# Two attention mixers woven into one list of steps: differential heads in pairs, a pair's neighbourhood tile between them, and other engine orders around it

## The reference

```python
zl = yl @ w_in; zc = yc @ w_in              # 9 groups of 256 columns
# pool: windowed mean, product with pool_w;  conv: gate, 31 taps, layernorm, silu, product with pw
# "diff": 4 heads, each two softmaxes of width 32
q, k = axial_rope(q) * scale, axial_rope(k)  # latent tokens alone
p = softmax(q @ [kl, kc].T)                  # 768 keys; 256 for context queries
o = (p[2h] - lam * p[2h+1]) @ v[h]           # v of width 64; then an rmsnorm per head
# "na": 4 heads of width 64, neighbourhood attention on the 8 x 64 grid
s = [q @ kl.T + bias (banded, -1e30 outside), q @ kc.T]
o = softmax(s) @ [vl, vc]
out = concat(pool, conv, diff, na) @ w_out
```

## Time and profile before

| | |
|---|---|
| median of 3 runs | 3031.3 us (3029.96 to 3033.0) |
| the profiled execution | 3028.46 us, of which the span 3026.8 us |
| granted PE clock over the span | 0.962 of 2.4 GHz |
| PE busy, DVE busy, ACT busy, POOL busy | 94%, 57%, 28%, 10% |
| layer 0: attention from its second step to mix_out | 835 to 1046 us |
| layer 1: the same | 2438 to 2591 us |

### The profile page before, as it was taken

The page is one execution under the profiler, slowest core; times in us unless marked ns, Lnnn a source line. Parts: engine busy times, 40 slices in busy tenths (PEclk is TensorE's granted clock), DMA queues, the critical chain, the costliest instruction groups (busy, mean ns, idle before and its releaser), DMA issues.

```text
span 3026.8 us, 39917 instructions
## 1 busy us (share of the span) xinstructions
PE 2851.0 (94%) x14770; PEld 2547.3 (84%) x14770; DVE 1723.1 (57%) x2888; ACT 856.7 (28%) x1147; POOL 291.6 (10%) x279
## 2 busy tenths in 40 slices
PE   6999999999779999999999899999998879999998
PEld 6999999979643489999999799999987844678887
DVE  7676677669663457666676772222247664533334
ACT  3221122241363332211221422112232264432222
POOL 0000000014322100000000100000004332000000
PEclk8999999999877999999999999999998979999999
DMA  5333333321220012332333232111212220123232
GB/s 202 118 118 123 114 118 132 108 75 55 62 61 7 18 52 98 131 130 93 132 123 120 76 112 74 59 63 62 72 47 91 67 66 7 56 83 105 89 98 83
DMA packets 63375, 264.95 MB, mean 88 GB/s; under 512 B 8880, under 2 KB 11824, under 8 KB 53680
## 3 DMA queue, kind: packets, MB, share of 16 engines
q1 hardware_dynamic: 50608, 180.17, 18.2%
q0 software_dynamic: 11520, 75.11, 7.6%
q10 hardware_dynamic: 1152, 8.39, 0.7%
HBM read 252.89 MB, written 2.10 MB: 84 GB/s over the span
## 4 chain that ended last, share of the span: by engine, by line
PE 82%; DVE 11%; ACT 4%; issue 2%; DMA 1%; POOL 0%; ACTq 0%; SPq 0%; DVEq 0%
PE ps L1453 73%; PE ps L1692 2%; DVE conv_acc L1206 2%; PE ps L1619 2%; PE ps L1647 1%; PE ps L1627 1%; DVE w_lo L954 1%; DVE rstd L1007 1%; DVE nmax L1311 1%; ACT e_sb L866 1%; DVE y_hi L1043 1%; DMA x<-in_xT 1%; DVE y_lo L1045 1%; ACT probs_t L880 1%; DVE mod_start_acc L1388 1%
## 5 line engine op out<-in xcount | busy, mean ns | idle before, releaser
L1453 PE MATMUL ps<-y_hi,w_hi 128*128 128x384 f32 (+2 forms) x3184 | 905.2, 347 | 66.2 <-DVE y_lo L1035 32.5
L1453 PE MATMUL ps<-y_hi,w_lo 128*128 128x384 f32 (+2 forms) x3184 | 893.8, 344 | 0.0
L1453 PE MATMUL ps<-y_lo,w_hi 128*128 128x384 f32 (+2 forms) x3184 | 893.3, 344 | 0.0
L1453 PEld LDWEIGHTS ps<-y_hi,w_hi 128*128 128x128 f32 x3184 | 582.5, 190 | 108.6 <-DVE y_lo L1035 36.9
L645 ACT ACTIVATE w_hi<-w_raw 128x1024 fp32r<-128x1024 f32 (+1 forms) x290 | 326.7, 1128 | 1048.7 <-PE ps L1453 1048.7
L1453 PEld LDWEIGHTS ps<-y_lo,w_hi 128*128 128x128 f32 x3184 | 585.9, 189 | 22.5
L1453 PEld LDWEIGHTS ps<-y_hi,w_lo 128*128 128x128 f32 x3184 | 585.7, 190 | 20.9 <-issue 0.2
L954 DVE TENSOR_TENSOR w_lo<-w_raw,w_hi 128x1024 fp32r<-128x1024 f32 (+1 forms) x290 | 386.5, 1333 | 311.7 <-ACT w_hi L645 308.5
L969 DVE SCALAR_TENSOR_TENSOR mod_acc<-mod_raw,cact,mod_acc 128x256 f32<-128x256 f32 x896 | 360.0, 477 | 0.0
L1453 PE MATMUL ps<-h_hi,w_hi 128*128 128x384 f32 (+2 forms) x1254 | 354.1, 342 | 0.0
L1453 PE MATMUL ps<-h_lo,w_hi 128*128 128x384 f32 (+2 forms) x1254 | 351.4, 339 | 0.0
(11 more groups left out here) (162 smaller groups left out, 2032.0 us busy)
## 6 DMA issues: line engine op xcount, KB each, us to landing
w_raw<-in_w_up SPq DMA_DIRECT2D x176, 512.0 KB, 3.5
mod_raw<-in_w_mod POOLq DMA_DIRECT2D x64, 1024.0 KB, 5.1
w_raw<-in_w_down SPq DMA_DIRECT2D x64, 704.0 KB, 4.1
w_raw<-in_w_in SPq DMA_DIRECT2D x36, 512.0 KB, 3.5
mod_start<-in_w_mod ACTq DMA_DIRECT2D x8, 1024.0 KB, 22.0
w_raw<-in_w_out SPq DMA_DIRECT2D x16, 512.0 KB, 3.5
stack<-qk_hi SPq DMA_DIRECT2D x48, 96.0 KB, 2.1
band<-in_rpb POOLq DMA_DIRECT2D x16, 224.0 KB, 6.5
```

The source lines that it names most:

```text
L1453: mm = pe.matmul(slot[s][:, at:at + b - a], w[s][:, k, :], r[:, k, a:b], start=(k == 0 and n == 0), stop=(k == kc - 1 and n == 2))
```

## The change

It redraws the mixer in both layers:

- `attention_steps` weaves: for each pair of heads c, the rows of queries in turn; each row gives a step of diff head 2c, one of diff head 2c+1, and one of the na pair c. The last two na rows of a pair follow at its end. An na step is now two heads and one tile. The counts of steps (36 and 24) and of turned tiles (48 and 32) stay.
- na scores (`near_scores`) alternate the two heads, which lie on partitions 0 to 63 and 64 to 127, and come behind the step's turns and value products on PE. Diff scores stay ahead of them.
- Value products (`weigh_values`) are made per pair of heads and tile, three steps behind, 128 queries at a time; the two heads write PSUM partitions 0 to 63 and 64 to 127 in turn. The probabilities lie in a ring of four tiles. ACT copies each result out (`copy_out`, now 24 and 16 small copies in place of 4 and 4 large ones).
- DVE takes a step's first maximum ahead of the last step's reciprocals.
- `Z_ORDER` makes NA_V, NA_K, NA_Q the last units in that order. DVE's rotary steps move from units 15 and 16 to units 9 and 11, with fewer taps there (`TAPS`); the na scaling moves behind the value copies.
- The high parts of diff chunks 0 and 2 are made on ACT ahead of unit 14, `qk_lo` of them on POOL ahead of the bands' masks, and head 0's stacks can go out during mix_in. Head 1's wait for the turned values, head 2's and 3's for the last scores of heads 0 and 1.
- The convolution's root, reciprocal, norm, silu and pointwise product and the pool product move into the steps. So do the first four `y_hi`.

```diff
 def attention_steps(with_ctx):
-    for h in range(HEADS):
-        tiles = [(t, False) for t in range(LAT // P)] + [(t, True) for t in range(CTX // P)] * with_ctx
-        out += [("diff", h, (t,), c, n == len(tiles) - 1) for n, (t, c) in enumerate(tiles)]
-    for h in range(HEADS):
-        tiles = [((0, 1), False), ((2, 3), False)] + [((0, 1), True)] * with_ctx
-        out += [("na", h, t, c, n == len(tiles) - 1) for n, (t, c) in enumerate(tiles)]
+    rows = [(t, False) for t in range(LAT // P)] + [(t, True) for t in range(CTX // P)] * with_ctx
+    for c in range(WC):
+        near = [("na", c, t, ctx) for t, ctx in rows]
+        for n, (t, ctx) in enumerate(rows):
+            out += [("diff", 2 * c, t, ctx), ("diff", 2 * c + 1, t, ctx)]
+            if n < len(rows) - 2:
+                out.append(near[n])
+        out += near[len(rows) - 2:]
     return out
...
+Z_ORDER = [CONV_A // 2, CONV_G // 2, POOL_U // 2, DIFF_Q // 2, DIFF_K // 2, DIFF_V // 2, NA_V // 2, NA_K // 2, NA_Q // 2]
+QK_AT = 7
+TAPS = (5, 6, 6, 6, 6, 6, 1, 6, 1, 6, 6, 6, 1)
...
             def stack_heads(layer):
                     if h == 1:
-                        sp.wait_ge(sems["conv_pw"], WC * (layer + 1))
+                        sp.wait_ge(sems["v_turned"], (layer + 1) * (TOK // P))
                     if h >= 2:
-                        sp.wait_ge(sems["scores"], scored + (h - 1) * per_head)
+                        sp.wait_ge(sems["scores"], scored + 2 * last_step(layer, "diff", h - 2) + 2)
+                    if h == 3:
+                        sp.wait_ge(sems["conv_pw"], WC * (layer + 1))
...
             def mix_in(p):      # DVE
-                    if u >= 3:
-                        convolve(6)
-                    if u == 15:
+                    if u >= 3 and u - 3 < len(TAPS):
+                        convolve(TAPS[u - 3])
+                    if u == 9:
...
                 for k in range(len(steps) + 3):      # DVE
+                    if k < len(steps):
+                        maxima(k, 0)
                     if 1 <= k <= len(steps):
                         invert_sums(k - 1)
-                    if k < len(steps):
-                        maxima(k, 0)
                     if k < len(steps):
                         maxima(k, 1)
                     if 1 <= k <= len(steps):
                         scale_probs(k - 1)
+                    if 1 <= k <= parts:
+                        if k == 1:
+                            t.wait("conv_sqrt")
+                        part = slice(CTX * (k - 1), CTX * k)
+                        dve.reciprocal(rstd[:, part], rstd[:, part]).then_inc(sems["conv_rstd"], 1)
...
+                def near_scores(k):      # PE
+                    kind, c, tile, ctx = steps[k]
+                    for a, b in spans(TOK)[1 if ctx else 0:]:
+                        for s in range(2):
+                            if a == 0 or ctx:
+                                t.wait("exp")
+                            rows = slice(DH * s, DH * s + DH)
+                            mm = pe.matmul(slot[s][:, a:b], z[rows, NA_Q + c, at:at + P], z[rows, NA_K + c, a:b],
+                                           start=True, stop=ctx or a > 0)
...
+                        for s in range(2):
+                            mm = pe.matmul(slot[s][:, 0:LAT], backward[:, :], bands[2 * c + s][:, j:j + GRID_H, :], start=False, stop=True)
+                            mm.then_inc(sems["scores"], 1)
...
+                def weigh_values(k):
+                    pe.wait_ge(sems["probs_t"], 2 * n_pair + 2)
+                    at = 512 * (n_pair % 2)
+                    for n_key, key in enumerate(keys):
+                        for s in range(2):
+                            col = (0 if kind == "diff" else W) + DH * (2 * c + s)
+                            mm = pe.matmul(outs[DH * s:DH * s + DH, at:at + P], v_sb[:, key, col:col + DH],
+                                           ring[(2 * n_pair + s) % 4][:, n_key, :], start=(n_key == 0), stop=(key == TOK // P - 1))
+                    mm.then_inc(sems["pv"], 1)
...
                     for s in range(2):
-                        if k < len(steps):
-                            scores(k, s)
-                        if turned and s < len(turned[2]):
+                        if k < len(steps) and not near:
+                            diff_scores(k, s)
+                        if turned and s < tiles_of(turned):
                             transpose_probs(k - 2, s)
-                            tiles_turned += 1
-                    if k == 0:
-                        conv_pointwise()
+                    if closed and closes_pair(closed):
+                        weigh_values(k - 3)
+                    if near:
+                        near_scores(k)
+                    if k < WC:
+                        pool_product(k)
+                    if k - pointwise_at in range(WC):
+                        conv_pointwise(k - pointwise_at)
```

More of the change, by code:

```diff
@@ L568, in mixer @@
+                low_parts((0, 2))
                 t.wait("band_raw", 16 * 2 * (HEADS - 1))
-                for h in range(HEADS - 1):
+                for h in (0, 1, 3):
                     for row in range(2):
                         mask_band(h, row)
[L573 to L577, removed]
@@ new lines, in mixer @@
+                steps = attention_steps(layer < LAYERS - 1)
+                for k, (kind, h, tile, ctx) in enumerate(steps):
+                    if k == last_step(layer, "diff", 1):
+                        pool.wait_ge(sems["stacked1"], 16 * 12 * (2 * layer + 1))
+                        load_band(2)
+                    if k == last_step(layer, "diff", 1) + 3:
+                        t.wait("band_raw", 16 * 2)
+                        mask_band(2, 0)
+                    if k == last_step(layer, "diff", 1) + 4:
+                        mask_band(2, 1)
@@ L869, in copy_probs @@
[L869 to L881 removed]
+                qk_hi_part(layer, 1)
@@ L1331, in scale_probs @@
                 def scale_probs(k):
-                    kind, h, tiles, ctx, _ = steps[k]
+                    kind, h, tile, ctx = steps[k]
                     keys = slice(LAT, TOK) if ctx else slice(0, TOK)
@@ L1367, in mixer @@
+                for first, c in norm_from.items():
+                    for j in range(parts):
+                        if first + j >= len(steps) + 3:
+                            if j == 0:
+                                t.wait("head_sqrt")
+                            head_norm(c, slice(CTX * j, CTX * j + CTX))
+                dve.wait_ge(sems["turned"], turned_before(layer + 1))
                 for m in range(DC):
                     t.wait("y_hi")
+                    if m == DC // 2:
+                        dve.wait_ge(sems["pv"], turned_before(layer + 1) // 2)
@@ L1596, in scores, with conv_pointwise @@
-                def scores(k, s):
-                    kind, h, tiles, ctx, _ = steps[k]
+                def conv_pointwise(m):
+                    if m == 0:
+                        t.wait("conv_act", WC)
+                    pe.wait_ge(sems["probs_t"], made[0])
+                    for a, b in spans(n):
+                        for c in range(WC):
+                            mm = pe.matmul(turn[:, a:b], pw_sb[:, c, P * m:P * m + P], (act_buf, hid_buf)[c][:, a:b],
+                                           start=(c == 0), stop=(c == WC - 1))
+                    mm.then_inc(sems["conv_pw"], 1)
@@ L1621, in scores @@
-                    if band:
-                        if tile == 0:
-                            t.wait("band_ready")
-                        j = GRID_H - 2 - 2 * tile
-                        mm = pe.matmul(slot[s][:, 0:LAT], backward[:, :], bands[h][:, j:j + GRID_H, :], start=False, stop=True)
-                    mm.then_inc(sems["scores"], 1)
-                steps = attention_steps(with_ctx)
-                pe.wait_ge(sems["rope_done"], layer + 1)
-                heads, norm_at, sqrt_at, pv_from = 0, None, None, None
```

490 lines of the change are left out of this document (238 added, 252 removed).

## The result

The changed kernel took 3065.8 us (median of 4 runs, 3064.2 to 3069.3), the kernel before 3032.1 us beside it: a ratio of 1.0119, 95% interval 1.0104 to 1.0134. It is slower by 34 us where 66 us of gain were predicted. The profiled execution has a span of 3062.5 us against 3026.8: 35.7 us to find.

A forecast was written before the change was run, and what follows sets the result against it. Diff steps were taken as bound by a two-slot loop, na steps by nearly full PE. Gains of 42.1 us (layer 0) and 24.6 (layer 1), 66.7 together, took 3028.5 to 2961.8, 2965 us on the median's footing; range 2925 to 3022.

The forecast's parts named there:

- G: Time of one woven latent triple (diff, diff, na): 9.8 + 2P + S = 14.3 us, 15.8 with surcharge; break-even at 20.0.
- 0.5 us for that score: First part of the triple: second diff step's second score, two turns of 0.67 us and two sets of value products.
- S: Both heads' na scores in a triple: 1.7 us with overlap in PE's array, 2.98 one after another.
- 6.0 us of slot loop: Rest of the triple after the bands: scores, maxima, copies and exponentials of two diff steps passing through two PSUM slots.
- I cost it at nothing: DVE's maximum ahead of reciprocals: a late na score delays reciprocals wanted two steps later; nothing, or 0.4 us a triple uncovered.
- surcharge of 1.5 us on G: Share for queueing and slow clock, a tenth or more as in the old na steps, raising 14.3 to 15.8 us.
- 8 in each layer: Count of woven latent triples, entering both layers' sums as 8G = 126.4 us.
- start of attention: Earlier rotary steps, value turns and stacks bring step 1's scores forward: 18.7 us gained in layer 0, 12.7 in layer 1.
- P: A pair's value products, 24 passes of 128 columns: 1.4 us with overlap in PE's array, 2.7 one after another.
- rival without overlap: Opposite halves of PE's array run one after another: G 18.2 to 19.7 us, total 3003 to 3027 us; chance 0.22.
- stall at the change to heads 2 and 3: Scores wait for stack transfers on SP's queue in layer 0: 1 us for head 2 and 4 for head 3.
- slower rival: Short value products no longer lift PE's clock: G up to 23.6 us; about 3057 us at G = 21.7; chance 0.08.

The follow-up runs named there:

- sums first: The changed kernel with DVE's order alone put back, the last step's reciprocals ahead of the step's first maximum: 3052.0 us, ratio 1.0075.

## Why the prediction was wrong

**The step that failed** is the size of G, the woven triple, and in it first the line that begins "0.5 us for that score" and ends "The copies and scalings that these wait for fit between them". It counts from the second diff step's second score over two turns and two sets of value products to the na scores, and makes it 4.6 us. In the six intervals of layer 0 this measured 10.4, 12.4 (with pointwise products), 9.3, 9.5, 8.3 and 8.9 us. PE's timeline in the triple above:

```profile
997.88 0.99 PE L1627 MATMUL ps<-stack,stack 96*128 96x512 f32 x2
1000.16 1.51 PE L1666 MATMUL ps<-ident,e_sb 128*128 128x128 f32 x6 [1.29 <-ACT probs_t L857]
```

From 997.88 to the na scores at 1006.80 it is 8.9 us, 4.3 over the forecast. PE waits 1.3 us for ACT's copy, which did not fit between; in the other intervals it waits 1.3 to 2.1 us for that copy or for POOL's half. The score, the first turn and the first set of products ran at the lower level of the clock: 0.99, 1.51 and 2.76 us, where 0.6, 0.9 and 1.46 stand elsewhere. The other part of the triple, from the na scores to that second score, took 10.8 us against 9.7 (S, the bands and the 6.0 us of slot loop). 14.3 + 4.3 + 1.1 = 19.7, the measured 19.8.

What both parts leave out is the order of the queues. They count as if each turn, maximum, copy and scaling could start when its engine was free. Three queues in strict order don't allow that: the near scores are last in PE's, their maximum is ahead of the diff step's reciprocals in DVE's, and POOL's half, DVE's half and PE's turn hang on these reciprocals. The turn in its place is ahead of the next diff score. That is a ring through four engines, with nothing of the next triple in it early. "I cost it at nothing" for DVE's order was the other half of the same mistake. What the runs put in its place: near scores first gave 49 us, sums first 14, and both together 34.

The surcharge of 1.5 us on G was taken from na steps that had PE full. Layer 0 from step 1 took 233.3 us against 187.4, 45.9 too much. The four intervals without pointwise products and norm, which the sum books apart, average 20.9 us, 5.1 over the forecast of 15.8; an estimate from these rows for eight triples is 41 of the 45.9 us. In layer 1 it was 189.5 against 141.4. There the count was wrong too: the list weaves all but the last two na rows of a pair. With no context rows in layer 1 only two of four rows are woven, and the last two follow one another (near scores 8 us apart), so "8 in each layer" holds for layer 0 alone.

**Right:** the start of attention, 29.2 us gained against 31.4 (3.9 short in layer 0 and 1.7 over in layer 1, so the sum is closer than its parts). The overlap: S was 1.49 against 1.7 and P 1.46 against 1.4, so the rival without overlap is out. It is fuller than "only the second pass of one head and the first of the other meet": the products of the two heads start in pairs, 0.01 us apart. These durations bear out the Trainium skill (TensorE: Matmul & The Clock Gate, Part 3), by which matmuls in different row or column groups run at the same time. The mode changes that the Trainium skill (TensorEngine Tiling (Array Packing), Key Properties) warns of show no cost here beyond these durations. The stall at the change to heads 2 and 3 is there: the chain has a transfer of 5.35 us from 920.99 until the score at 926.47, against 5 predicted.

**Too small:** in layer 1 the transfers. POOL waits for the last tap (2407 us) before it loads bands and only then makes low parts (2412.7), so SP issued 24 stack transfers in a row from 2415.83; step 1 waited 5.8 us. The tail was put at 5 us and the second pair's norm at 4 and 3 us of path, as if steps were left to cover it. In layer 0 the chain has 12.8 us between the last value product, ended at 1040.9, and mix_out; PE's wait for y_lo there is 8.6 us, in layer 1 7.1.

**The slower rival** gave the place of the decision, G = 20, and a time near the measured one (3057), but for the clock alone. The clock fell in its direction (0.74 and 0.76, from 0.80 and 0.89), and more of the triple is clock than the forecast had: on the chain above a score of 1.01 us, turns of 1.55 and 1.51 and products of 2.76 are some 3.0 us longer than the same work at the upper level (0.6, 0.89 twice, 1.46). But computing the short value products twice raised the clock by 0.04 or less, and the order of PE's queue alone, with the same products, moved it by 0.05 over 820 to 1020 us and the time by 49 us. So that the order brought on the loss is shown; how it divides into waits and clock is not. The chance of 0.08 was too low because only one mechanism stood for everything that makes G longer than 20.

## What to carry to other kernels

When steps of two kinds are woven through engines that each run in order, write down for each engine what stands ahead of the piece that others wait for longest, and follow the ring once around all engines; a sum of busy times with a surcharge doesn't see it. Whether a producer's piece should go ahead of older work is a question for pairs of queues: the same DVE order gained 9 us in one kernel, cost 14 in another, and gained 14 once PE's order was put right. Here the packing and the earlier start did what was said of them, and the weave neither paid nor cost much; the place of one call decided between 1.0119 and 0.9959.

## What the runs showed of the hardware that was not expected

- Products over 64 rows for two heads, on opposite halves of the array, overlap wholly: 1.49 us for both against 1.49 for one, and 1.50 when all of one head's are issued ahead of the other's.
- For 64 columns each, 24 passes of 128 columns take 1.46 us alternating, 2.38 us one head after the other. There only four of a head's twelve products ran beside one of the other head; a head's near scores are four products and overlapped in full. How many products can lie between two that overlap was not varied by itself.
- DVE's scaled sum of two SBUF tensors (128x768) took 1.02 us alone and 2.82 us beside a POOL mask of 2.1 us in SBUF.
- A turn or value product in the same place ran at both levels of the clock, turns 0.89 and 1.51 us, products 1.46 and 2.76 us, within 4 us of one another (granted clock 0.50 and 1.00), with 0.74 in the mean of the stretch; computing the products twice raised it only from 0.73 to 0.77.
